# Two transformer stacks in one kernel: the long-convolution filter moves from the start into the second FFN, loads are reordered, and activation tables are loaded at other places

## The reference, cut to what matters

```python
cond = jax.nn.silu(c)
m = (cond @ w_mod[l] + b_mod[l]).reshape(bsz, 3, 3, D_MODEL)
x = x + 0.5 * m[:, 0, 2][:, None] * swiglu(adaln_in(x, ...), w1, w3, w2)
```

```python
h = jnp.sin(fq * (z @ w1 + b1))            # z: 256 x 33, w1: 33 x 64
h = jnp.sin(fq * (h @ w2 + b2))            # w2, w3: 64 x 64
h = jnp.sin(fq * (h @ w3 + b3))
h = (h @ w4).reshape(L, 2, CONV_WIDTH)     # w4: 64 x 1024
h = h * jnp.exp(-t[:, :, None] * deltas)
kfull = concatenate([h[:, 0], 0, h[:0:-1, 1]])
return kfull * lax.rsqrt(sum(kfull * kfull) + EPS)
```

## Time and profile before

| | us |
|---|---|
| three runs | 2209.54, 2214.69, 2221.80; median 2214.69 |
| profiled execution | 2210.28, its span 2208.4 |
| PE busy in it | 1998.1 (90%) |
| DVE busy | 1386.2 (63%) |
| ACT busy | 978.3 (44%) |
| POOL busy | 48.4 (2%) |
| chain that ended last | 83% of the span on PE, 9% on DVE, 5% on ACT |

### The profile page before, as it was taken

The page is one execution under the profiler, slowest core; times in us unless marked ns, Lnnn a source line. Parts: engine busy times, 40 slices in busy tenths (PEclk is TensorE's granted clock), DMA queues, the critical chain, the costliest instruction groups (busy, mean ns, idle before and its releaser), DMA issues.

```text
span 2208.4 us, 38356 instructions
## 1 busy us (share of the span) xinstructions
PE 1998.1 (90%) x16574; PEld 1672.6 (76%) x16582; DVE 1386.2 (63%) x2130; ACT 978.3 (44%) x1611; POOL 48.4 (2%) x47
## 2 busy tenths in 40 slices
PE   4999879899899984799989999598998999898998
PEld 1788666788788772578878879367887888657887
DVE  5987874777777765556665555645555555555554
ACT  3454444444544540344444454334445444544443
POOL 4400000000000000000000000000000000000000
PEclk7999989999999996899999999699999999999999
DMA  7787552588588560336645545104554555403552
GB/s 289 307 337 304 192 228 106 185 305 318 197 319 305 203 258 0 143 134 229 229 159 196 202 160 208 69 11 155 195 202 165 199 202 200 157 17 113 200 201 79
DMA packets 54131, 423.88 MB, mean 192 GB/s; under 512 B 5939, under 2 KB 5987, under 8 KB 26539
## 3 DMA queue, kind: packets, MB, share of 16 engines
q1 hardware_dynamic: 52028, 413.49, 49.8%
q0 software_dynamic: 1936, 7.95, 1.0%
HBM read 420.29 MB, written 1.13 MB: 191 GB/s over the span
## 4 chain that ended last, share of the span: by engine, by line
PE 83%; DVE 9%; ACT 5%; DMA 2%; POOL 1%; issue 1%; SPq 0%; DVEq 0%; ACTq 0%
PE pw L401 16%; PE pw L403 16%; PE pw L402 16%; PE acc L401 8%; PE acc L402 8%; PE acc L403 8%; PE pw L551 2%; PE acc L586 2%; PE pssq L452 2%; PE pw L554 2%; ACT ring_hi L785 2%; DMA land<-stream 1%; PE acc L572 1%; DVE ring_lo L956 1%; DVE rs L876 1%; ACT L751 1%
## 5 line engine op out<-in xcount | busy, mean ns | idle before, releaser
L401 PE MATMUL pw<-h_hi,ring_hi 128*128 128x256 bf16 x3280 | 903.5, 275 | 60.3 <-DVE h_lo L945 30.1
L402 PE MATMUL pw<-h_lo,ring_hi 128*128 128x256 bf16 x3280 | 904.6, 276 | 0.0
L403 PE MATMUL pw<-h_hi,ring_lo 128*128 128x256 bf16 x3280 | 904.4, 276 | 0.0
L956 DVE TENSOR_TENSOR ring_lo<-land,ring_hi 128x1024 bf16<-128x1024 f32 x633 | 743.1, 1228 | 171.7 <-ACT ring_hi L785 171.5
L785 ACT ACTIVATE ring_hi<-land 128x1024 bf16<-128x1024 f32 x633 | 619.4, 1041 | 41.2 <-PE acc L403 24.0
L401 PEld LDWEIGHTS pw<-h_hi,ring_hi 128*128 128x128 bf16 x3280 | 322.2, 98 | 127.4 <-issue 66.4
L401 PE MATMUL acc<-a_hi,ring_hi 128*128 128x256 bf16 x1408 | 384.8, 273 | 4.4 <-DVE a_lo L987 4.4
L402 PE MATMUL acc<-a_lo,ring_hi 128*128 128x256 bf16 x1408 | 384.9, 273 | 0.0
L403 PE MATMUL acc<-a_hi,ring_lo 128*128 128x256 bf16 x1408 | 384.8, 273 | 0.0
L403 PEld LDWEIGHTS pw<-h_hi,ring_lo 128*128 128x128 bf16 x3280 | 324.7, 99 | 40.9
L402 PEld LDWEIGHTS pw<-h_lo,ring_hi 128*128 128x128 bf16 x3280 | 322.7, 98 | 37.5 <-issue 0.3
(11 more groups left out here) (182 smaller groups left out, 1450.5 us busy)
## 6 DMA issues: line engine op xcount, KB each, us to landing
land<-stream SPq DMA_DIRECT2D x211, 1536.0 KB, 6.5
modw<-wmod SPq DMA_DIRECT2D x144, 512.0 KB, 7.8
biasT<-bias_rows POOLq DMA_DIRECT2D x3, 1536.0 KB, 11.6
biasT<-bias_rows POOLq DMA_DIRECT2D x1, 3072.0 KB, 11.7
cst_s<-cst SPq DMA_DIRECT2D x1, 1792.0 KB, 10.1
x<-xT SPq DMA_DIRECT2D x1, 1024.0 KB, 12.2
out<-proj SPq DMA_DIRECT2D x1, 1024.0 KB, 3.9
par_s<-par SPq DMA_DIRECT2D x1, 795.0 KB, 7.1
```

Source lines behind the costliest of these rows:

```text
L401: mm(o, lhs[0], rhs[0], start=start, stop=False, skip_group_check=True)
L402: mm(o, lhs[0], rhs[1], start=False, stop=False, skip_group_check=True)
L403: return mm(o, lhs[1], rhs[0], start=False, stop=stop, skip_group_check=True)
L956: v.tensor_tensor(ring_lo[:, t % RING, b, :], land[:, t % LAND, b, :], ring_hi[:, t % RING, b, :], ALU.subtract).then_inc(lo_ready, 1)
```

## The change

- The filter's layers and taps leave the start. In stage i = 2 PE does layer l at the head of slot 3, 6 or 9 and tap n at the head of slot 12 to 15, DVE follows at the end of the same slot, ACT takes the sine one slot later and loads Silu's table again behind it. DVE does POOL's former work, the bias and frequency of a layer, and the decay straight out of PSUM. The sums come in slot 16, the squares on ACT in slot 17, their sum in slot 18. The norm and spectrum move to stage i = 4, "cd", with ACT's root ahead of its copy of chunk 7.
- `par`, and the one-hot constants, are loaded behind x and the first four modulation blocks; zT and the decay are loaded in stage 2, into sq.
- Modulation groups: 6 in stage 0 (4 before), none in stage 1 (2), 3 in stage 2 (4), 6 in stage 3 (4), none in stage 4 (1), one in stage 5 as before.
- In FFNs and in "sw" ACT loads the table of Silu or Exp behind the norm's eight high parts, not ahead of them. One more Silu is at the very start.

```diff
-MOD_AT = {0: [[]] + spread(2, 6, 20) + [[]], 1: spread(6, 8, 6), 2: [[]] + spread(8, 12, 20) + [[]],
-          3: [[]] + spread(12, 16, 20) + [[]], 4: spread(16, 17, 6), 5: [[]] + spread(17, 18, 20) + [[]]}
+MOD_AT = {0: [[]] + spread(2, 8, 20) + [[]], 2: [[]] + spread(8, 11, 20) + [[]],
+          3: [[]] + spread(11, 17, 20) + [[]], 5: [[]] + spread(17, 18, 20) + [[]]}
+LAYER_AT, TAP_AT = (3, 6, 9), (12, 13, 14, 15)
...
         def _(sp):
             sp.dma_start(condb[:], bass.AP(crow.tensor, 0, [[0, P], [1, D]])).then_inc(cond_in, 16)
-            sp.dma_start(par_s[:], par).then_inc(par_in, 16)
-            sp.dma_start(cst0_s[0:33, 0:SMALL], cst0[0:33, 0:SMALL]).then_inc(cst0_in, 16)
...
             sp.dma_start(x[:], xT).then_inc(x_in, 16)
+            sp.dma_start(par_s[:], par).then_inc(par_in, 16)
+            sp.dma_start(oh_s[0:33, :], cst0[0:33, 0:HOT]).then_inc(cst0_in, 16)
...
+                    if i == 2 and n == 0:
+                        sp.wait_ge(ssq_ready, 3)
+                        sp.dma_start(late_s, cst0[:, HOT:CST0_W]).then_inc(decay_in, 16)
...
+            def filter_tap(n):
+
+                pe.wait_ge(filt_act, 3)
+                if n:
+                    pe.wait_ge(taps_out, n)
+                mm(pfil[:], fh(2)[:, (n % 2) * P:(n % 2 + 1) * P], pa("fw4", (n // 2) * 512, 512, 64),
+                   start=True, stop=True).then_inc(filt_mm, 1)
...
                 for j in range(2, NFF):
+                    if i == 2 and j in LAYER_AT:
+                        filter_layer(LAYER_AT.index(j))
+                    if i == 2 and j in TAP_AT:
+                        filter_tap(TAP_AT.index(j))
                     down(j - 2)
                     up(j)
...
                 root(("norm", n), rs[:])
-                if n < NSTAGE:
-                    kind = STAGES[n][0]
-                    if kind in ("ffn", "sw"):
-                        warm(ACT.Silu if kind == "ffn" else ACT.Exp)
...
+                if n < NSTAGE and STAGES[n][0] in ("ffn", "sw"):
+                    warm(ACT.Silu if STAGES[n][0] == "ffn" else ACT.Exp)
...
                 if kind == "ffn":
                     for j in range(NFF):
                         silu(ffn_no[i], j)
+                        if i == 2 and j - 1 in LAYER_AT:
+                            filter_layer(LAYER_AT.index(j - 1))
+                            warm(ACT.Silu)
+                        if i == 2 and j == TAP_AT[-1] + 2:
+                            filter_squares()
...
+                    if kind == "cd" and c == 7:
+                        root("filter", norm_c)
                     act.wait_ge(proj_mm, proj_no[i] + c + 1)
...
+            def filter_layer(l):
+
+                dve.wait_ge(filt_mm, 5 + l)
+                done(v.tensor_scalar(ft(0), pfil[0:64, 0:S], pa("fb", l, 1, 64), pa("ff", 0, 1, 64), ALU.add, ALU.mult))
+
+                done(v.tensor_scalar(ft(1), ft(0), 1 / (2 * math.pi), MAGIC, ALU.mult, ALU.add))
+                done(v.tensor_scalar(ft(1), ft(1), MAGIC, None, ALU.subtract))
+                done(v.scalar_tensor_tensor(ft(2), ft(1), -TWO_PI_HI, ft(0), ALU.mult, ALU.add))
+                done(v.scalar_tensor_tensor(ft(2), ft(1), -TWO_PI_LO, ft(2), ALU.mult, ALU.add))
+                v.tensor_scalar(ft(0), ft(2), 3.1415925, -3.1415925, ALU.min, ALU.max).then_inc(filt_dve, 1)
+
+            def filter_tap(n):
+
+                dve.wait_ge(filt_mm, 8 + n)
+                v.tensor_tensor(f_taps[:, n // 2, n % 2, :], pfil[:], c0("decay", (n % 2) * 512, 512), ALU.mult).then_inc(taps_out, 1)
...
                 for j in range(1, NFF - 1):
                     mods(i, j)
                     gated(j)
+                    if i == 2 and j in LAYER_AT:
+                        filter_layer(LAYER_AT.index(j))
+                    if i == 2 and j in TAP_AT:
+                        filter_tap(TAP_AT.index(j))
+                    if i == 2 and j == TAP_AT[-1] + 1:
+                        filter_sums()
+                    if i == 2 and j == TAP_AT[-1] + 3:
+                        filter_squares()
...
                 else:
-                    if kind == "ab":
-                        filter_norm()
-                        filter_spectrum()
                     early = -(-MIXERS[kind]["chunks"] // 3)
                     for t in range(FIRST[i], FIRST[i] + early):
-                        mods(i, t - FIRST[i])
                         split_low(t + AHEAD)
+                        if kind == "cd" and t == FIRST[i]:
+                            filter_norm()
+                            filter_spectrum()
```

More of the change, by code:

```diff
@@ L52 @@
            Si=512, causal=512)
-CST0 = dict(zT=256, oh=2048, decay=1024)
-SMALL = 2304
+CST0 = dict(oh=2048, zT=256, decay=1024)
+HOT = 2048
 def offsets(widths):
@@ L209, in c0 @@
             o, full = CST0_AT[name]
-            return cst0_s[0:rows, o + i:o + i + (full if w is None else w)]
+            return late_s[0:rows, o - HOT + i:o - HOT + i + (full if w is None else w)]
         accv = acc[:].rearrange("p (k s) -> p k s", s=S)
@@ L323, in _ @@
             g = nc.gpsimd
-            steps = [0]
-            def done(ins):
-                steps[0] += 1
-                ins.then_inc(pool_step, 1)
-                pool.wait_ge(pool_step, steps[0])
             g.memset(eps_col[:], EPS)
@@ L384, in _ @@
                                    ).then_inc(bias_in, 16)
-                if before is None:
-                    filter_sums()
             pool.wait_ge(bias_in, 64)
@@ L487, in ffn @@
                 if i == 0:
-                    pe.wait_ge(taps_out, 4)
+                    pe.wait_ge(rows_ready, 4)
                 for b in range(4):
@@ L615, in head_norms @@
             def head_norms(step):
[L617 removed]
+                if step == 2:
+                    pe.wait_ge(spectrum_ready, 1)
                 pe.wait_ge(mix_dve, step)
@@ L712, in _ @@
             act.wait_ge(zeros_set, 1)
+            fn(warmed[:], ones[0:1, 0:1], ACT.Silu)
             act.wait_ge(cond_in, 16)
@@ L717, in _, with filter_squares @@
                 fn(f_rows[0:n, which, :], acc[0:n, which * 512:(which + 1) * 512], ACT.Copy, scale=8.0).then_inc(rows_ready, 1)
-            act.wait_ge(fbf_ready, 1)
             def filter_layer(l):
-                act.wait_ge(filt_mm, 5 + l)
-                fn(ft(0), pw[0][0:64, 0:S], ACT.Identity, scale=pa("ff", 0, 1, 64), bias=fbf[:, l:l + 1]).then_inc(filt_act, 1)
                 act.wait_ge(filt_dve, l + 1)
                 fn(fh(l), ft(0), ACT.Sin).then_inc(filt_act, 1)
-            def filter_taps():
-                for d in range(2):
-                    for tt in range(TT):
-                        act.wait_ge(filt_mm, 8 + 2 * d + tt)
-                        fn(f_taps[:, d, tt, :], acc[:, (2 * d + tt) * 512:(2 * d + tt + 1) * 512], ACT.Copy).then_inc(taps_out, 1)
+            def filter_squares():
+                act.wait_ge(sums_set, 1)
+                fn(f_sq, f_sq, ACT.Square).then_inc(filt_act, 1)
             def root(what, t):
-                act.wait_ge(recip_ready, 3 if what == "filter" else what[1] + 1 + (what[1] > 1))
+                act.wait_ge(recip_ready, 6 if what == "filter" else what[1] + 1 + (what[1] > 4))
                 fn(t, t, ACT.Sqrt).then_inc(root_ready, 1)
@@ L794, in _ @@
             squares(0)
-            for l in range(3):
-                filter_layer(l)
             split_high(0)
@@ L801, in _ @@
                     split_high(1)
-                    filter_taps()
-                if kind == "ab":
-                    act.wait_ge(filt_mm, 13)
-                    root("filter", norm_c)
                 if kind == "ffn":
@@ L1139, in _ @@
                 for k in range(KD):
+                    if (g, k) == (0, KD - 1):
+                        sinks()
                     mod_block(g, k)
```

86 lines of the change are left out of this document (28 added, 58 removed).

## The result

The changed kernel takes 2241.26 us in the median of its runs (2236.28 to 2246.15), the kernel before 2213.82 us in the same session: a ratio of 1.0128, with a 95% interval of 1.0111 to 1.0146, 27.4 us slower. The profiled execution took 2246.15 us (span 2244.4), 36.0 us more by span than the profile of before (2208.4). The changed kernel was run again later in another session (label e9_again): 2236.57 us against 2214.12, ratio 1.0098 (1.0085 to 1.0112), span 2236.0. Both profiles are used here, since they differ in one instructive place. VectorE is DVE in the rows and ScalarE is ACT; a stand is a stretch in which an engine has its next instruction and waits for another engine or a load.

What follows compares the result with a forecast made beforehand. PE was taken as the bound between norm and sum of squares, losing time only by standing still or extra work. Terms -3.5 - 2.9 - 10.7 - 5.8 + 31.8 + 3.6 + 9.5 = +22.0 on 2214.7 gave 2237 us, range 2220 to 2250.

Steps and rivals of the forecast that it cites:

- The taps: Second FFN (i = 2): PE waits for DVE's previous tap, three stands of 6.6 us, 19.8, plus 6.9 of clock.
- The clock term: Second FFN: PE's clock falls behind each of three stands, costing 2.3 us a time, 6.9 in all.
- The filter's work on PE: Second FFN: three filter layers add 1.4 us and four taps of 512 columns 3.7 us on PE.
- The "cd" stage: Filter's norm and spectrum there: DVE waits for ACT's root, a weight load goes late, PE stands; +9.5 us (0 to +12).
- The "ab" stage: Modulation blocks and spectrum leave it, so PE no longer stands for late weights in the projection; -10.7 us (-8 to -12).
- FFN i = 0 and i = 3: With 48 blocks DVE falls behind PE; net -2.9 us in the first with the filter gone, +3.6 in i = 3.
- The rival that the transfers bind: In the two FFNs with 48 blocks DVE waits 0.3 us a slot for weight splits; +12, 2249 us; chance 0.12.
- The start: Before the first norm: the filter's wait goes, but a later sum of squares delays the last modulation loads; -3.5 us (-8 to 0).
- The wait for the sum of squares: Start: the bias table lands last, so the sum of squares ends near 31.2 in place of 23.7 and DVE waits.
- the ceiling of 8 us: Start: without the filter the first norm could begin at 43.0, 8 us less; as a rival 2232 us, chance 0.08.
- Silu's table: Table load moved behind the norm's high parts saves 0.73 us at seven further FFNs and "sw"; -5.8 us (-3 to -6.6).
- the row: The trace's 1.28 us for a table load, taken over the skill's 2.66 with drain; the drain rival had chance 0.02.

Runs made afterwards that it cites:

- e9_again: The changed kernel, unaltered, run a second time in a later session: 2236.57 us against 2214.12 for the kernel before, ratio 1.0098.

## Why the prediction was right, and where it was not

- **The taps** (three stands of 6.6 us and 2.3 us of clock behind each, 26.7 together). Right, shown by moving them: 6.55 us three times, 28.1 with the clock. The clock term was a little small: 28.1 - 19.65 = 8.4 in place of 6.9 (7.5 by the second profile, whose stage is 1.0 shorter).
- **The filter's work on PE**, 1.4 and 3.7. With the taps behind, 185.6 - 179.7 + 0.7 for the table is 6.7, against 5.1: 1.6 too small. ScalarE's silus, slot by slot against the kernel before, show where: each layer puts them 0.68 us later and each tap 1.16, 2.0 and 4.6 in all. The prediction had counted 0.47 for a layer and 0.93 for a tap.
- **The "cd" stage**, +9.5. Right in mechanism and size: 61.98 - 52.7 = +9.3 in the projection; VectorE's stand, the late load and PE's stand come in the order forecast. Moving the root took 8.0 of it.
- **The "ab" stage**, -10.7. The projection lost 11.0, of which the blocks alone are 3.0 and the spectrum with the blocks behind it 8.0. The first profile hides it under a longer stretch at half speed in the attention; the second, without that stretch, has -11.2 for the whole stage.
- **FFN i = 0 and i = 3** with 48 blocks, VectorE the bound: +2.7 against +2.9 in i = 3, shown by giving the blocks back (-3.3). VectorE's waits for ScalarE's silu in i = 3 fall from 15.3 us to 1.7. In i = 0 -1.7 or -1.2 against -2.9: the blocks cost 5.4 there (forecast 4.5), and with 32 blocks the stage is 7.1 shorter than before (forecast 6.7 + 0.7). The rival that the transfers bind was wrong: in i = 3 neither ScalarE nor VectorE waited for a transfer, in i = 0 ScalarE once, for 0.86 us (1.1 in the second profile).
- **The start**, -3.5. This is the step that failed: -0.6, and the first norm's piece at 50.32 where 47 was given as the sign. "Four whose loads are issued from 34.6 on and land from about 38.2 to 42.2": they were issued from 33.4 on and the last landed near 45.2. I had taken the removal of POOL's filter work for cheaper work on VectorE alone and not seen that POOL's next instruction, a table load of 1.5 MB, moved up with it from behind the filter to 32.66, among those loads. Holding it gave 2.0 us of the 2.9 missing; the rest stays open. The wait for the sum of squares was forecast (31.2, measured 30.07), and the ceiling of 8 us too: with the order of before the norm begins 8.4 us before its old time.
- **Silu's table**, -5.8 over eight norms. The last low part ends 0.72 us earlier in the modulated norms, as the rows said, and 0.63 in the others. What reached the stage was 0.7 in i = 2 (first silu 10.37 behind the norm's start before, 9.65 after), 0.3 to 0.4 in i = 3, 5 and 8, 1.5 to 1.8 in i = 6 and 9 with the clock, and in i = 11 0.3 against the kernel before, nothing against the tables in front. Why it is 0.7 in one norm and 0.3 in another wasn't settled. The seven later stages came near the forecast as a sum, not one by one: hy, for which nothing was forecast, got 1.5 shorter, i = 6 and 9 gained 1.9 and 1.7, and sw has -1.4 in one profile and +2.3 in the other. The Trainium skill ("ScalarE: Activation LUTs", What ACT_TABLE_LOAD costs) counts a drain on top of the load, 2.66 us with it; where the clock is the same on both sides nothing near 1.38 us more came back, so the measurement speaks for the row.
- **The sum.** +22.0 forecast; +27.6 and +35.9 by the two pairs of profiles, +27.4 and +22.5 by the medians of the two sessions. The pair at +35.9 holds the long stretch at half speed in ab that is worth some 13 us. The pair at +27.6 misses the forecast by 5.6, which is start +2.7, first FFN +1.7, second FFN +2.0, the seven later stages +0.8, less 0.5 each in ab, i = 3 and cd and rounding. The profiled execution of before lay 3.5 to 4 us under the medians of its kernel, so that the medians differ by less. That the forecast of 2237 lies so near 2241.26 and 2236.57 is therefore in part luck; the terms are off by more, though the two large ones, the taps and ab, are right in mechanism and size.

What stays open is what decides when the clock rises in ab's attention. PE's two idle stretches ahead of it are alike (5.8 and 6.6 us in the first profile), and the low stretch is 27.3, 30.7 or 54.6 us in kernels that are identical up to there.

## What to carry to other kernels

Before two engines pass a single buffer back and forth inside a pipelined loop, look where in its slot each of them issues its part: PE's product at the head of a slot and VectorE's answer at the slot's end made every turn wait for nearly a whole slot's work, 28 us for three turns, and moving two lines removed it. When work leaves an engine's queue, ask what stood behind it in that queue, transfers above all, and what it will now run into. Filler work belongs in stages with slack per slot, counted in blocks: 40 in an FFN were free here and 48 cost 3.3 and 5.4 us; 8 in a mixer were free and 16 cost 3.0.

## What the runs showed of the hardware

- PE's granted clock stayed at half speed for very different times behind like idle: from 27.3 to 54.6 us in ab's attention, in kernels with the same work and the same stands there. Two profiles of one kernel can so differ by 13 us in one stage, and a comparison of two profiles should be checked for it window by window.
- What half speed costs depends on what PE does in it: in ab's attention 27.3 us of it in place of 3.4 cost 2.0 to 2.5 us, each us beyond 27.3 about 0.5, and each head that fell into that part took 7.35 us in place of 3.95.
- After a norm's idle of PE the low clock lasts 3.4 or 6.8 us with nearly the same idle, so that a norm's low parts ready 0.63 us earlier show as 0.3 us or as 1.8.
- Around three stands of 2.5 us the clock was low for 6.8, 0 and 3.4 us, around three of 6.5 us for 10.2, 6.8 and 10.2, and in the second profile of the same kernel for 10.2, 6.8 and 6.8.
